# Output projection as seven block products per four pairs, with weight sums on GpSimd, and the second half of its weights loaded early

## The reference

```python
h = rmsnorm(x, norm1_g[l])
u, q, k, v, g_pool, g_attn = jnp.split(h @ w_in[l], SPLITS, axis=-1)
y_pool = multiscale_pool(u, pool_w[l], pool_scale[l]) @ w_pool_proj[l]
y_attn = sliding_window_attention(q, k, v, sinks[l], rel_bias) @ w_attn_proj[l]
mixed = jax.nn.sigmoid(g_pool) * y_pool + jax.nn.sigmoid(g_attn) * y_attn
x = x + mixed @ w_out[l]
x = x + moe(rmsnorm(x, norm2_g[l]), w_router[l], b_router[l], w_up[l], b_up[l],
            w_down[l], b_down[l])
return rmsnorm(x, final_g)
```

## Time and profile before

| | |
|---|---|
| time, median of 3 runs | 1080.56 us (1079.85 to 1082.23) |
| the profiled execution | 1079.79 us, its span 1078.0 us |
| PE busy | 1015.9 us, 94% of the span |
| granted TensorE clock, mean | 0.986 of 2.4 GHz |
| DVE / ACT / POOL busy | 267.3 / 103.9 / 61.4 us |
| moved by DMA | 430.03 MB, mean 399 GB/s |
| chain that ended last | PE 78%, DMA 18%, issue 2% |

### The profile page before, as it was taken

The page is one execution under the profiler, slowest core; times in us unless marked ns, Lnnn a source line. Parts: engine busy times, 40 slices in busy tenths (PEclk is TensorE's granted clock), DMA queues, the critical chain, the costliest instruction groups (busy, mean ns, idle before and its releaser), DMA issues.

```text
span 1078.0 us, 11897 instructions
## 1 busy us (share of the span) xinstructions
PE 1015.9 (94%) x5112; PEld 483.7 (45%) x5112; DVE 267.3 (25%) x642; ACT 103.9 (10%) x229; POOL 61.4 (6%) x57
## 2 busy tenths in 40 slices
PE   9999999999999999989989898989899989998997
PEld 8999985333333333333333333333333333333332
DVE  3543333212131212121203022121212120313021
ACT  2140012101010101000000001010100000000012
POOL 2354300200000000000000000000000000000001
PEclk9999999999999999999999999999999999999999
DMA  9905998999999999999999999999999999999996
GB/s 335 355 3 179 411 386 327 420 422 427 429 436 426 427 430 436 431 431 429 429 433 432 430 430 429 435 429 432 431 430 435 427 425 427 427 427 429 424 418 238
DMA packets 38307, 430.03 MB, mean 399 GB/s; under 512 B 6204, under 2 KB 7917, under 8 KB 19181
## 3 DMA queue, kind: packets, MB, share of 16 engines
q1 hardware_dynamic: 33792, 427.04, 94.0%
q10 hardware_dynamic: 4156, 1.14, 0.5%
q0 software_dynamic: 304, 1.06, 0.3%
HBM read 428.17 MB, written 1.06 MB: 398 GB/s over the span
## 4 chain that ended last, share of the span: by engine, by line
PE 78%; DMA 18%; issue 2%; ACT 1%; DVE 0%; POOL 0%; SPq 0%; POOLq 0%; DVEq 0%; ACTq 0%
PE bank L1173 29%; PE bank L1180 22%; DMA ring<-in_w_down 14%; PE bank L1153 5%; PE bank L943 5%; PE bank L1107 4%; DMA ring<-in_w_up 4%; PE bank L1017 3%; PE bank L953 3%; PE bank L874 2%; PE bank L1136 1%; PE bank L1146 1%; PE bank L888 1%; ACT h_buf L771 1%; PE bank L842 0%
## 5 line engine op out<-in xcount | busy, mean ns | idle before, releaser
L1173 PE MATMUL bank<-ring,z_buf 128*64 128x512 f32 x2032 | 455.6, 600 | 20.0 <-issue 15.2
L1173 PEld LDWEIGHTS bank<-ring,z_buf 128*64 128x64 f32 x2032 | 148.0, 138 | 310.9 <-issue 310.6
L1180 PE MATMUL bank<-ring,h_buf 128*64 128x512 f32 x960 | 220.5, 613 | 30.9 <-DMA ring<-in_w_down 20.1
L1180 PEld LDWEIGHTS bank<-ring,h_buf 128*64 128x64 f32 x960 | 72.4, 141 | 158.5 <-issue 142.3
L1691 DVE COPY y<-bank 128x256 f32<-128x256 f32 x32 | 12.1, 419 | 273.5 <-PE bank L1180 273.5
L1107 PEld LDWEIGHTS bank<-u_buf,m_buf 128*128 128x128 f32 x512 | 59.7, 192 | 21.9 <-issue 21.9
L1107 PE MATMUL bank<-u_buf,m_buf 128*128 128x128 f32 x512 | 65.3, 281 | 0.0
L1699 DVE TENSOR_SCALAR swi<-bank 128x256 f32<-128x256 f32 x64 | 27.2, 424 | 146.2 <-PE bank L1173 141.2
L1660 DVE TENSOR_TENSOR z_buf<-bank,g2x 128x512 f32<-128x512 f32 (+1 forms) x33 | 22.3, 675 | 165.4 <-PE bank L1107 164.3
L1153 PE MATMUL bank<-y,u_buf 128*128 128x512 f32 x120 | 54.1, 594 | 0.0
L656 POOL TENSOR_TENSOR m_buf<-acc,ring 128x512 f32<-128x512 f32 x2 | 2.5, 1273 | 860.3 <-DVE acc L1669 860.2
(11 more groups left out here) (215 smaller groups left out, 587.5 us busy)
## 6 DMA issues: line engine op xcount, KB each, us to landing
ring<-in_w_up SPq DMA_DIRECT2D x40, 4096.0 KB, 24.4
ring<-in_w_down SPq DMA_DIRECT2D x20, 4096.0 KB, 21.9
ring<-in_w_up SPq DMA_DIRECT2D x38, 2048.0 KB, 27.6
ring<-in_w_down SPq DMA_DIRECT2D x11, 2048.0 KB, 19.8
ring<-in_w_down SPq DMA_DIRECT2D x20, 1024.0 KB, 17.8
ring<-in_w_up SPq DMA_DIRECT2D x18, 1024.0 KB, 9.8
ring<-in_w_in SPq DMA_DIRECT2D x5, 2048.0 KB, 23.2
ring<-in_w_down SPq DMA_DIRECT2D x10, 512.0 KB, 20.6
```

What stands on the lines that cost most here:

```text
L1173: ins = nc.tensor.matmul(up_banks[j][e * SLOTS:(e + 1) * SLOTS, :], xgT[:, k, e * SLOTS:(e + 1) * SLOTS], row[:, j * CH:(j + 1) * CH], sta ...
L1180: ins = nc.tensor.matmul(banks[n][e * SLOTS:(e + 1) * SLOTS, :], of[:, k, e * SLOTS:(e + 1) * SLOTS], w[e].rearrange("p (k n) -> p k n", k ...
```

## The change

The output projection is computed as seven block products in place of eight. With W11, W12 (low input half; first and second output half), W21, W22 (high input half) and the tokens split in two halves, GpSimd makes four sums of weights (`out_sums`, each four ops of 128x512 for four output chunks), DVE four sums of activations (`mixed_sums`), PE makes seven kinds of product, each for four output chunks (16 matmuls of 128x128 with 128 columns), and DVE combines them out of four banks.

- PE: 112 matmuls with 128 columns instead of 64 with 256. The logits take chunks in the order 4 to 7, 0 to 3. The squares are summed by ten small products instead of four.
- POOL: 16 ops of 128x512, which begin when both halves of w_out have landed and stand behind its last sum for gate pair 7. They write into slots 1 (`C_KV`), 2 (`C_Q`) and 0 (`C_U`).
- DVE: t1, t2, t4, t3 (the sums of `mixedT`), a copy of the first bank (`p1`), then the copy of x to `x1T` as before, then the combining, with two reductions of squares in place of six additions.
- SP: `W_OUT1` goes to slot 3 (`C_GP`) and is loaded after gate pair 2. The expert loads change their order and wait for the sums and products that now use their slots.

Diff, cut to its core:

```diff
+W_OUT1 = R + C_GP
...
+            sp.wait_ge(unit_done, UNIT[f"gate{LAST_POOL - 1}b"] + 1)
+            load_rows(W_OUT1, w_out[0][CH:D, :])
+
             sp.wait_ge(unit_done, UNIT["attn1"] + 1)
...
-            for load in (2, 3, 0, 4, 6, 5, 1, 8, 9, 10):
+            for load in (3, 4, 6, 5, 8, 9, 0, 1, 2, 10):
                 slot = slot_of(FIRST, load)
                 sp.wait_ge(unit_done, UNIT[last_use[slot]] + 1)
-                if load == 5:
-                    load_rows(W_OUT1, w_out[0][CH:D, :])
-                if slot == C_Q:
-                    sp.wait_ge(mixed_ready, KD)
-                if slot == 8:
+                if slot == C_GA2:
                     sp.wait_ge(xT_moved, 2)
                 if slot == W_OUT0:
-                    sp.wait_ge(w_out0_done, 1)
+                    sp.wait_ge(out_done, 1)
+                    sp.wait_ge(out_sum_ready, 12)
+                if slot == C_KV:
+                    sp.wait_ge(out_done, 3)
+                    sp.wait_ge(out_sum_ready, 16)
+                if slot == C_Q:
+                    sp.wait_ge(out_done, 5)
+                    sp.wait_ge(x1T_ready, 4)
+                if slot == C_GP:
+                    sp.wait_ge(out_done, 6)
                 load_expert(slot, load, FIRST)
...
+            pool.wait_ge(*load_at(W_OUT0))
+            pool.wait_ge(*load_at(W_OUT1))
+            w_low, w_high = (ring[:, n % R, :].rearrange("p (k n) -> p k n", n=D) for n in (W_OUT0, W_OUT1))
+            for i in range(4):
+                if i == 2:
+                    pool.wait_ge(unit_done, UNIT[f"gate{PAIRS - 1}b"] + 1)
+                if i in (1, 3):
+                    pool.wait_ge(out_sum_ready, 4 * i if i == 1 else 8)
+                for c in range(4):
+                    first, second = slice(c * P, (c + 1) * P), slice((c + 4) * P, (c + 5) * P)
+                    one, other, how = ((w_low[:, :, second], w_high[:, :, second], ALU.add),
+                                       (out_sums[0][:, c], w_low[:, :, first], ALU.subtract),
+                                       (w_low[:, :, first], w_low[:, :, second], ALU.subtract),
+                                       (w_high[:, :, first], out_sums[1][:, c], ALU.subtract))[i]
+                    nc.gpsimd.tensor_tensor(out_sums[i][:, c], one, other, how).then_inc(out_sum_ready, 1)
...
+            out_blocks(0, lambda c: w_low[:, :, c * P:(c + 1) * P], m_low[:, :, 0:P], True, False)
+            pe.wait_ge(mixed_sum_ready, 1)
+            out_blocks(2, w_sum(0), t1, True)
+            pe.wait_ge(mixed_sum_ready, 2)
+            out_blocks(1, w_sum(1), t2, True, False)
+            pe.wait_ge(*load_at(W_OUT1))
+            pe.wait_ge(mixed_ready, KD)
+            pe.wait_ge(out_read, 1)
+            out_blocks(0, lambda c: w_high[:, :, c * P:(c + 1) * P], m_high[:, :, 0:P], False)
+            pe.wait_ge(out_read, 3)
+            pe.wait_ge(mixed_sum_ready, 4)
+            out_blocks(1, w_sum(2), t3, False)
+            out_blocks(3, lambda c: w_high[:, :, (c + 4) * P:(c + 5) * P], t4, True)
...
             mix(PAIRS - 1)
...
+            nc.vector.tensor_tensor(t2, m_high[:, :, P:SEQ], t1, ALU.subtract).then_inc(mixed_sum_ready, 1)
+            p1, u = pre
+            dve.wait_ge(out_done, 1)
+            nc.vector.tensor_copy(p1, out_of(0)).then_inc(out_read, 1)
+            dve.wait_ge(mixed_sum_ready, 2)
+            nc.vector.tensor_tensor(t4, t2, m_high[:, :, 0:P], ALU.subtract).then_inc(mixed_sum_ready, 1)
+            nc.vector.tensor_tensor(t3, m_high[:, :, P:SEQ], m_low[:, :, P:SEQ], ALU.subtract).then_inc(mixed_sum_ready, 1)
 
             dve.wait_ge(unit_done, UNIT[f"gate{PAIRS - 1}b"] + 1)
             nc.vector.tensor_copy(x1T[:, 0:KD // 2, :], xT[:, 0:KD // 2, :]).then_inc(xT_moved, 1)
```

More of the change, by code:

```diff
@@ L106, in count_landed @@
 def count_landed():
-    loads = [len(range(slot, MIXER_LOADS, R)) for slot in range(R)]
+    loads = [1 + (slot == W_OUT1 % R) for slot in range(R)]
     at = {}
@@ L223, in hybrid_block_kernel @@
         bmap = swi[0:N_BUCKETS + 1, 0:3 * WINDOW]
[L224 removed]
+        x1sq = swi[:, 0:2 * SEQ].rearrange("p (k s) -> p k s", k=KD // 2)
         sq_sum = swi[:, 2 * SEQ:3 * SEQ].rearrange("p (t s) -> p t s", t=TT)
@@ L737, in _, with square_x1 @@
             link(nc.scalar.activation(warm, eps, ACT.Sqrt))
[L738 to L743, removed]
+            def square_x1(dst, of):
+                nc.scalar.activation(dst, of, ACT.Square).then_inc(x1sq_ready, 1)
+            act.wait_ge(out_read, 4)
+            square_x1(x1sq, x1T[:, 0:4, 0:P])
+            act.wait_ge(x22_ready, 1)
+            act.wait_ge(x1sq_added, 1)
+            square_x1(x1sq, x1T[:, 4:8, P:SEQ])
+            act.wait_ge(x1T_ready, 4)
+            square_x1(x1sq_first, x1T[:, 4:8, 0:P])
+            act.wait_ge(x1sq_added, 2)
+            for lo, hi in ((0, 2), (2, 3), (3, 4)):
+                act.wait_ge(x1T_ready, 4 + hi)
+                square_x1(x1sq[:, lo:hi, :], x1T[:, lo:hi, P:SEQ])
             act.wait_ge(unit_done, UNIT["squares"] + 1)
@@ L1013, in _ @@
             outs = [begin(f"outT{i}") for i in range(4)]
[L1015 to L1018, removed]
-            pe.wait_ge(*load_at(W_OUT0))
[L1021 to L1024, removed]
@@ L1025, in _, with out_block @@
-            ins.then_inc(w_out0_done, 1)
+            w_low, w_high = (ring[:, n % R, :].rearrange("p (k n) -> p k n", n=D) for n in (W_OUT0, W_OUT1))
+            m_low, m_high = mixedT[:, 0:KD // 2, :], mixedT[:, KD // 2:KD, :]
+            t1, t2, t4, t3 = (mixed_sums[:, i] for i in range(4))
+            def out_block(dst, w, rows, opens, closes=True):
+                for k in range(KD // 2):
+                    ins = nc.tensor.matmul(dst, w[:, k, :], rows[:, k, :], start=(opens and k == 0), stop=(closes and k == KD // 2 - 1),
+                                           skip_group_check=True)
+                return ins
@@ new lines, in out_blocks, with w_sum, of @@
+            def out_blocks(to, of, rows, opens, closes=True):
+                for c in range(4):
+                    ins = out_block(outs[to][:, c * P:(c + 1) * P], of(c), rows, opens and c == 0, closes)
+                ins.then_inc(out_done, 1)
+            def w_sum(i):
+                def of(c):
+                    pe.wait_ge(out_sum_ready, 4 * i + c + 1)
+                    return out_sums[i][:, c]
+                return of
+            pe.wait_ge(*load_at(W_OUT0))
+            pe.wait_ge(mixed_ready, 4)
```

127 lines of the change are left out of this document (81 added, 46 removed).

## The result

The changed kernel takes 1085.43 us (median of 7 runs, 1083.91 to 1086.85), the kernel before in the same comparison 1080.89 us (1079.85 to 1082.23, 7 runs): ratio 1.0041, 95% interval 1.0029 to 1.0053. It is slower by 4.5 us, beyond the upper end of my range, 1083.8 us. The profiled execution has a span of 1084.4 us against 1078.0. A place in one trace can be set against the same place in another to about 1 us only: 16 matmuls near 6 us from the start take 2.03 us in the trace before, 2.19 in the one after and up to 3.07 in others, and everything behind them is shifted by it.

The account below looks back on a forecast made before the run. The load stream's gapless start was taken as the bound: 177.75 us against 176.8, 1.0 us later, PE's 1.7 us gain being spent waiting. Added to the median 1080.56 us: 1081.6 us, range 1077.8 to 1083.8 us.

Parts of the forecast that it names:

- What bounds the kernel: Load stream, continuous from 200 us to the end: the moment its gaps stop, 176.8 us before the change, sets the end.
- The early load costs nothing where it stands, and its price is paid in the queue behind: Near 78 us DMA is idle, so free; two expert loads, 9.8 us of work, leave the stretch from 98.22 us.
- DVE and GpSimd take turns: From 134 us DVE's operations with two SBUF inputs wait for GpSimd's sums; the copy of x ends at 143.15 us.
- the root on ACT comes 1.7 us earlier: End of projection: PE gains 2.6 and 0.5 us, pays 1.35 for six small products; half loads issued at 171.75 us.
- my own price of a turn: A DVE operation with two SBUF inputs ends 0.55 us after GpSimd's current one; each turn delays GpSimd by 0.45 us.
- Against 176.8: 1.0 us later: Gapless start of the load stream: the second aside half is in at 177.75 us, against 176.8 before.
- the sum's rule: Load 8, issued at 143.2 us, lands at 150.8; later loads follow gapless to 177.75, so its delay moves the end one for one.
- thin stretch: The 8 us after the stream's restart at 176.15 us run at 396 instead of 428 GB/s, little being queued: 0.6 us.
- PE does not suffer: PE wants loads 0 and 1 at 168 us (here 165.5) and load 2 at 177 us (here 170.4).
- Rival (c): DVE beside GpSimd misses one more turn, 1.7 us on the copy of x, load 8 and the end: 1083.3 us; chance 0.2.
- signs that I had named for being right: Among them: up product 1.7 us earlier, PE's load waits about 2.7 us longer, DMA never idle after 141 to 145 us.
- seven and a half: Loads 8, 9, 0, 1, 2, 10 and half of the aside load, behind load 5, needing 31.85 us of DMA.

Follow-up runs that it names:

- the early load alone: The kernel before with only the second half of w_out loaded after gate pair 2 and expert load 2 moved to the list's end: 1081.18 us, ratio 1.0001.
- the kernel with sums without reading: The changed kernel with GpSimd's 16 sums of weights replaced by writes of zero of the same size: 1080.54 us, ratio 0.9999.
- ten squares in the kernel before: The kernel before with six more one-column products behind its first two for the squares, ten in all: 1086.36 us, ratio 1.0041.
- the kernel with four squares: The changed kernel with four small products for the squares instead of ten, DVE adding up the rest: 1084.48 us, ratio 1.0037.
- the one with six: The changed kernel with DVE's half of the copy of x on ACT and six products for the squares instead of ten: 1081.27 us, ratio 0.9998.
- narrow matmuls: The kernel before with each output projection matmul of 256 columns split in two of 128: 1081.86 us, ratio 1.0012.
- the three changed kernels with four: The changed kernel with four square products, 1084.48 us; also with x's copy on ACT and router weights late, 1080.97; also with DVE's scratch in z_buf, 1079.26.

## Why the prediction was wrong

**What bounds the kernel: right.** The end follows what the load stream has moved by 200 us, and so the moment at which it stops having gaps, within 1.5 us in all kernels of the table.

**The early load costs nothing where it stands, and its price is paid in the queue behind: right**, and the early load alone brought nothing (within 0.1%).

**DVE and GpSimd take turns: right.** The copy of x ended 1.05 us later than I had stepped through: the last mix missed one turn more than I gave it (ended at 137.5, forecast 136.35). The rule of the Trainium skill ("SBUF — State Buffer", the part on the shared port pair) that a copy in a two-port mode is locked out too agrees with this trace: the copy of x took 1.75 us beside GpSimd sums, and 0.69 us and 0.68 us (the kernel with sums without reading) with GpSimd idle. No run here has that copy beside a GpSimd write.

**"PE: the root on ACT comes 1.7 us earlier": this step failed.** It came 2.5 us later (166.18 for 163.67 us) and the first up row 5.3 us later. I followed DVE's turns up to the copy of x and stopped there, since that decides load 8. The chain went on: two small operations, then two additions from a bank, then `u`, which the fifth kind of product waits for. By my own price of a turn the two small ones had to end near 146 us and `u` near 148, and the fifth kind was due at 147. I wrote that each kind gives DVE 3.57 us and counted its operations at 0.69. And the clock stood nowhere in the prediction. The six more small products were costed at 1.35 us, by their duration; the runs show that with ten of them the clock comes down, which cost 2.8 us in the changed kernel's trace and 4.3 of the 5.6 us of ten squares in the kernel before. The first fall, 1.7 us behind PE's wait, I cannot put down to anything: the kernel with four squares has the same wait and no such fall.

**"Against 176.8: 1.0 us later": mis-sized.** With PE's first row where it was before, load 8 at 144.74 us costs 3.5 us (2.6 to 5.5 by the interval of the ratio). By the sum's rule the 1.5 us over 143.2 in load 8 give 2.5 us. Most of the remaining 1.0 us is the rate: I let the refill run at 428 GB/s and booked 0.6 us against the kernel before for a thin stretch that a full queue would not have. The rows of that kernel:

```profile
core 0: us, PE busy (x) PEld busy (x) DVE busy (x) ACT busy (x) POOL busy (x), PEclk, DMA share, GB/s
152.00:170.00 18.00, 17.94 (x155) 15.61 (x156) 10.23 (x31) 6.47 (x12) 0.00 (x0) 1.00 1.01 430
170.00:180.00 10.00, 10.00 (x50) 3.75 (x48) 1.89 (x7) 2.02 (x4) 0.00 (x0) 1.00 1.00 397
180.00:200.00 20.00, 20.00 (x102) 7.75 (x100) 7.24 (x29) 1.21 (x3) 0.00 (x0) 1.00 1.01 420
```

The stretch at 397 GB/s is there with a full queue as well (DMA's share is 1.00), and it costs 0.7 us; so the thin stretch was no matter of how much is queued. DMA's share of 0.99 beside the 396 GB/s in the earlier trace rows said so already. The last 0.3 us are within the scatter.

**"PE does not suffer"** held for its loads, none of which it waited for ahead of 200 us, and failed for its own work. **Rival (c)** (one more turn, 1083.3 us) had the right sign and the nearest number, but its step hardly came: the copy ended at 144.2 us, under (c)'s own 144.3, and (c) too left PE's lateness out. Of the marks that I had set for "wrong", none fired (load 8 before 141 or after 145 us, an empty queue before loads 1 or 10, PE waiting for loads 0 to 2): I had set no such mark on the first up row. Three of the signs that I had named for being right did fail: the up product began 5.3 us later instead of 1.7 earlier, PE's waits for loads did not grow, and DMA ran thin once more, at 225 GB/s from 178 to 182 us, since the first half load came so late. (The "seven and a half" later loads of the prediction are six and a half; its sum of 31.85 us counts them so.)

## What to carry to other kernels

Where a kernel has a bound late in its span, reduce every early edit to one question, when does that stream become gapless, and ask it of both things that can hold it: the queue of loads and the engine whose step releases the next one. If two engines take turns at SBUF, step the slower one through to the last instruction that anybody waits for, not to the one you are curious about. And count tiny matmuls at more than their time: ten where four had stood put the tensor clock to its lower level here, which then stretched everything behind them.

## What the runs showed of the hardware

- Ten products of one column instead of four, among a handful of others of 32 columns, brought TensorE's granted clock from 2.4 to 1.2 GHz with PE busy throughout (4.00 of 4.00 us in 164 to 168 us). That is of ten squares in the kernel before. All six profiles of kernels with ten products have such a fall between 162 and 176 us, the one with six has it too, and none of the six with four (before, early load alone, narrow matmuls, and the three changed kernels with four). Probably not in every execution: the runs of ten squares form two groups, and only one of the slow group was profiled.
- Matmuls of 128 columns in place of 256, 128 of them in the projection, did not bring it down. Behind a wait of PE of 1.88 us it fell in one profile (at 150 us, to 0.50) and did not in another.
- A VectorE copy from SBUF to SBUF of 1024 elements per partition took 1.75 us beside GpSimd sums and 0.68 us with GpSimd idle; a copy of 128 elements 1.34 us and 0.27 us. An addition of 512 elements with both inputs in SBUF took 1.61 us beside GpSimd sums and 0.69 us beside GpSimd writes.
- A load of 2.10 MB issued into an empty DMA queue landed after 7.5 us (load 8, changed kernel) and 7.6 us (before, and load 8 of the kernel with sums without reading), 2.7 us more than its bytes at 428 GB/s; so an idle stretch costs more than its length.
